# Post-norm decoder trunk, two layers: front transfers, token-major units, router order and the last block of each expert rearranged

## The chip, the cores and the metric

The kernel runs on one core of one Trainium2 chip. The metric is the time of one execution on the device in microseconds (us), the median of three. TensorE multiplies matrices and writes PSUM, VectorE and ScalarE do elementwise work, GpSimd issues indirect transfers, and SyncE's queue issues nearly all loads.

## What is computed

A hybrid trunk of D_MODEL 1024 runs over 256 tokens and two layers. x is float32, and every large product must be of about float32 accuracy.

```python
x <- LayerNorm(ALPHA * x + TokenMixer(x))
x <- LayerNorm(ALPHA * x + ChannelMixer(x))   # layer 0: dense SwiGLU; layer 1: top-2-of-8 SwiGLU experts
hcat = x @ w_in      # q, kv, gates | conv | retention q, k, v, g | merge gates
y = native sparse attention, short gated convolution, multi-scale retention, each projected, gated, summed, projected
```

D_FF is 3584 for the dense layer and for each of the eight experts. The router's logits are x @ moe_router (1024 x 8); each token goes to its two largest, with the softmax of the two as weights. The sparse attention has compressed keys and values: blocks of 32 tokens at stride 16, with a position encoding added, go through a small MLP.

## The kernel before

**Weights.** The weights are one stream of tiles ("subs") of 128 x 2048 float32, 1 MB each, in the order of use. SyncE loads them into six raw slots and waits, for each, until the tile six before has been split. ScalarE rounds a tile to w_hi (two instructions of 1024 columns, L892 and L893) and VectorE subtracts to get w_lo (L1205, L1208), into three ring slots. Activations are split in the same way (xT_hi and xT_lo, act_hi and act_lo), and every product is three matmuls: high x high, high x low, low x high. A split waits until TensorE has used the tile three before. Every engine works in the order in which its program is written.

**Layers.** norm(n) normalises the tokens, in two tiles of 128 (t = 0, 1). to_features(n) transposes them on TensorE (L419) into feature-major xT. stay_busy(k) issues k dummy matmuls (L407) where TensorE would wait. A mixer is 46 steps s, one per sub: projection units (fm_unit: weights 128x128 stationary, xT moving, 256 token columns, lines 361 to 363), four compression steps (L462, L463) that read the z pieces of key and value, branch projections and the output projection. Attention and retention work stands between the two halves of the units. Values must be token-major for attention and retention; they are computed feature-major and transposed: values_to_tokens (L471, four transposes a layer), ret_values (L579, eight a layer), each followed by a ScalarE copy.

**Front.** SyncE issues x, the identity, subs 0 and 1, three transfers of constants, then subs 2 to 5. Sub 0 is split in quarters (L899, L1218), after x is transposed.

**Router.** After norm(3), router_logits takes the product with wr2 (the router's high and low columns, 16 in all) as stationary, adds the two parts with a second small product (log2_ps), and counts with products against a lower triangle and ones (L752 to L756). VectorE's routing() finds the maxima, the masks, the weights (after ScalarE's exponential), the positions, the picks of item 0 (L1662), and the extra items for experts with more than 128 tokens; n_items = 8 plus these. gather_first (L764) then gathers item 0's rows by matmul.

**Experts.** Each item is seven blocks of 512 hidden columns. A block has four gate and up subs (up_half, L375 to L377: 128 tokens stationary, 512 weight columns moving), four transposes of the hidden block (L805), a split of it into hT_hi (ScalarE, L1116) and hT_lo (VectorE, L1691), and a down product over two subs. In blocks 0 to 5 the transposes stand behind the next block's gate; the last block is:

```python
n = i * NB + (NB - 1)
hidden_transposes(n)
gathered(i + 1)
down(n, s0 + (FFN - 2), MOE0 + 4, False, True)
```

gathered transposes the next item's rows (L779), which GpSimd has gathered by an indirect transfer (L1191) during the item. The result y is split (L1152, L1720) and scattered by matmul (L846, L847) in the next item, and VectorE adds it to acc (L1713).

## Time and profile before

| | |
|---|---|
| Median of three runs | 1862.42 us (1861.42 to 1862.79) |
| Profiled execution | 1861.52 us, its span 1859.7 us |
| Granted TensorE clock, mean | 0.996 |
| Busy: TensorE, VectorE, ScalarE, GpSimd | 1825.2, 1464.5, 1177.4, 45.2 us |
| Moved by DMA | 511 MB, 275 GB/s |

Times are microseconds from the start of the span. A matmul's row shows the time from its start to the end of its results; matmuls overlap, so the step from one start to the next is what one costs. The stages: front to 30, layer 0's mixer to 302, its dense part to 547, layer 1's mixer to 848, router to 863, eight items to 1839, scatter, norm and output to the end.

### The profile page before, as it was taken

Reading aid. Unit: us, or ns where it says so; the run is one execution under the profiler, and the core shown is the slowest. Engines: PE = TensorE matmul, PEld = TensorE weight load, DVE = VectorE, ACT = ScalarE, POOL = GpSimd, SP = SyncE. Lnnn points to the kernel's source line nnn. Section 1 sums busy time; section 2 is a strip of 40 time slices with the busy share of each in tenths; the row PEclk is TensorE's granted clock in tenths of the full one; section 3 lists DMA queues with packets and bytes.
Section 4 is the critical chain, followed back from the end, with each engine's and each line's share of the span. In section 5 each row is a group of like instructions: output and inputs, shape, how many; then the busy total and the mean of one; then the engine's idle time right before and its main releaser. Section 6 shows DMA issues by size and latency. Waiting matters only on the chain.

```text
span 1859.7 us, 29640 instructions
## 1 busy us (share of the span) xinstructions
PE 1825.2 (98%) x10921; PEld 1588.7 (85%) x10925; DVE 1464.5 (79%) x1697; ACT 1177.4 (63%) x1448; POOL 45.2 (2%) x15
## 2 busy tenths in 40 slices
PE   8999999999999999999999999999999999999995
PEld 7999998999989999996888888888888888888884
DVE  5685577544567665768999989999999999999998
ACT  6554444444447444445777787787787877777874
POOL 0000000000000000000101001000010010100100
PEclk9999999999999999999999999999999999999998
DMA  9444445555537333455999999999999999999994
GB/s 384 182 159 137 163 178 182 183 192 190 180 136 269 140 139 137 160 201 192 370 375 350 380 350 375 371 342 385 372 352 379 346 377 375 335 387 368 361 368 172
DMA packets 71870, 511.07 MB, mean 275 GB/s; under 512 B 8064, under 2 KB 8192, under 8 KB 10880
## 3 DMA queue, kind: packets, MB, share of 16 engines
q1 hardware_dynamic: 68944, 498.10, 70.9%
q10 hardware_dynamic: 1280, 6.32, 0.9%
q0 software_dynamic: 1584, 5.77, 0.9%
q8 instruction: 46, 0.75, 0.2%
q14 instruction: 16, 0.13, 0.0%
HBM read 508.06 MB, written 2.10 MB: 274 GB/s over the span
## 4 chain that ended last, share of the span: by engine, by line
PE 95%; DVE 3%; DMA 1%; ACT 1%; issue 0%; SPq 0%; DVEq 0%
PE PS L375 19%; PE PS L377 18%; PE PS L376 18%; PE PS L361 11%; PE PS L362 10%; PE PS L363 10%; PE PS L805 1%; DMA raw<-wstream 1%; PE PS L531 1%; PE PS L563 1%; PE PS L546 1%; DVE X L1260 0%; PE PS L846 0%; PE PS L847 0%; PE PS L541 0%; DVE bst L1230 0%
## 5 line engine op out<-in xcount | busy, mean ns | idle before, releaser
L1205 DVE TENSOR_TENSOR w_lo<-raw,w_hi 128x1024 fp32r<-128x1024 f32 x471 | 575.7, 1222 | 229.9 <-ACT w_hi L892 229.0
L892 ACT ACTIVATE w_hi<-raw 128x1024 fp32r<-128x1024 f32 x471 | 499.1, 1060 | 282.2 <-PE PS L377 210.1
L1208 DVE TENSOR_TENSOR w_lo<-raw,w_hi 128x1024 fp32r<-128x1024 f32 x471 | 574.0, 1219 | 0.0
L893 ACT ACTIVATE w_hi<-raw 128x1024 fp32r<-128x1024 f32 x471 | 493.1, 1047 | 0.0
L361 PE MATMUL PS<-xT_hi,w_hi 128*128 128x256 f32 x1408 | 404.2, 287 | 0.2 <-DVE w_lo L1208 0.2
L362 PE MATMUL PS<-xT_lo,w_hi 128*128 128x256 f32 x1408 | 398.2, 283 | 0.0
L363 PE MATMUL PS<-xT_hi,w_lo 128*128 128x256 f32 x1408 | 398.2, 283 | 0.0
L375 PE MATMUL PS<-w_hi,xT_hi 128*128 128x512 f32 x896 | 355.0, 396 | 1.5 <-DVE xT_lo L1677 1.5
L377 PE MATMUL PS<-w_hi,xT_lo 128*128 128x512 f32 x896 | 349.5, 390 | 0.0
L376 PE MATMUL PS<-w_lo,xT_hi 128*128 128x512 f32 x896 | 348.9, 389 | 0.0
L361 PEld LDWEIGHTS PS<-xT_hi,w_hi 128*128 128x128 f32 x1408 | 269.6, 192 | 10.3 <-issue 8.2
L362 PEld LDWEIGHTS PS<-xT_lo,w_hi 128*128 128x128 f32 x1408 | 269.8, 192 | 0.2
L363 PEld LDWEIGHTS PS<-xT_hi,w_lo 128*128 128x128 f32 x1408 | 269.8, 192 | 0.0
L375 PE MATMUL PS<-w_hi,act_hi 128*128 128x512 f32 x624 | 244.6, 392 | 5.0 <-DVE act_lo L1691 5.0
L376 PE MATMUL PS<-w_lo,act_hi 128*128 128x512 f32 x624 | 243.0, 389 | 0.0
L377 PE MATMUL PS<-w_hi,act_lo 128*128 128x512 f32 x624 | 242.9, 389 | 0.0
L375 PEld LDWEIGHTS PS<-w_hi,xT_hi 128*128 128x128 f32 x896 | 168.2, 188 | 38.9 <-DVE w_lo L1208 4.2
L377 PEld LDWEIGHTS PS<-w_hi,xT_lo 128*128 128x128 f32 x896 | 168.1, 188 | 35.9
L376 PEld LDWEIGHTS PS<-w_lo,xT_hi 128*128 128x128 f32 x896 | 168.5, 188 | 33.2
L375 PEld LDWEIGHTS PS<-w_hi,act_hi 128*128 128x128 f32 x624 | 117.1, 188 | 32.8 <-issue 6.8
L377 PEld LDWEIGHTS PS<-w_hi,act_lo 128*128 128x128 f32 x624 | 117.2, 188 | 24.6
L376 PEld LDWEIGHTS PS<-w_lo,act_hi 128*128 128x128 f32 x624 | 117.1, 188 | 23.5
(266 smaller groups left out, 1429.8 us busy)
## 6 DMA issues: line engine op xcount, KB each, us to landing
raw<-wstream SPq DMA_DIRECT2D x472, 1024.0 KB, 6.7
soft<-ln ACTq DMA_DIRECT2D x4, 1024.0 KB, 5.6
X<-x SPq DMA_DIRECT2D x1, 1024.0 KB, 4.9
x_rows<-X ACTq DMA_DIRECT2D x1, 1024.0 KB, 5.0
out<-X ACTq DMA_DIRECT2D x2, 512.0 KB, 3.7
cst<-consts SPq DMA_DIRECT2D x1, 910.0 KB, 10.5
sm<-small SPq DMA_DIRECT2D x1, 729.0 KB, 12.3
rg<-constb SPq DMA_DIRECT2D x1, 337.0 KB, 10.9
```

The costliest lines, as they stand in the source:

```text
L361: mm(o, wh, rhs_hi[:, k, :], start=(k == 0), stop=False)
L362: mm(o, wh, rhs_lo[:, k, :], start=False, stop=False)
L363: last = mm(o, wl, rhs_hi[:, k, :], start=False, stop=(k == nk - 1))
L375: mm(o, lh, wh, start=(first and n == 0), stop=False)
L376: mm(o, lh, wl, start=False, stop=False)
L377: last = mm(o, ll, wh, start=False, stop=(final and n == len(ks) - 1))
L531: last = mm(o[par][:, i, 0:w], query(NR * g + 2 * i + par, qt), kT[par * DH:(par + 1) * DH, a, g, 0:w], start=False, stop=(i == 1), skip_g ...
L546: last = nc.tensor.transpose(PS[:, TB + kb, r * P:(r + 1) * P], prob[:, r, kb * P:(kb + 1) * P], ident)
L892: activate(w_hi[:, at % RING, 0:SUB // 2], src[:, 0:SUB // 2], ACT.Copy).then_inc(half_done, 1)
L893: activate(w_hi[:, at % RING, SUB // 2:SUB], src[:, SUB // 2:SUB], ACT.Copy).then_inc(hi_done, 1)
L1205: v.tensor_tensor(w_lo[:, at % RING, 0:SUB // 2], src[:, 0:SUB // 2], w_hi[:, at % RING, 0:SUB // 2], ALU.subtract)
L1208: v.tensor_tensor(w_lo[:, at % RING, SUB // 2:SUB], src[:, SUB // 2:SUB], w_hi[:, at % RING, SUB // 2:SUB], ALU.subtract).then_inc(lo_done, 1)
```

## The change

1. SyncE issues the identity first, x in two transfers, sub 0 in four, and the constants behind sub 3 in four transfers, with the position encoding (pos_in) behind sub 2. Sub 0's quarters are split as they land; VectorE does the first two between its xT_lo pieces.
2. Units 4, 16 and 17 (attention values, retention values) are computed token-major by tm_unit: xT stationary, 256 weight columns moving. The transposes of values and the ScalarE copies behind them go. The columns of w_in are reordered, so that unit 3 holds both keys and unit 4 both values.
3. The logits are computed by token: xT stationary, wr2 moving, with the high part of the first tokens before the second tokens' transposes. The dummies are recounted (12 to 9 before x, 2 and 8 new in the front, 16 to 9 in norm(3), 2, 9 and 8 to 7 and 4 in the router).
4. In routing, counts and picks come before the weights; one weight split is moved from norm(3) to behind the picks; the extras go to GpSimd; acc and the zero y go to ScalarE; gather_first is in two halves around the load of n_items; the first expert's first tile waits for the first half of the rows alone.
5. In each item's block 5 the down product issues the transposes of block 6 between its two subs; their split goes to hL_hi and hL_lo, ahead of the last weight split of that block on ScalarE and VectorE. One weight split stands ahead of two additions at the item's start.

```diff
+TOKEN_UNITS = (4, 16, 17)
...
-            sp.dma_start(X[:, :, :], x.rearrange("(t p) d -> p t d", p=P)).then_inc(x_in, 16)
-            sp.dma_start(ident, consts[:, C_ID:C_ID + P]).then_inc(x_in, 16)
-            for t in range(RAW):
+            sp.dma_start(ident, consts[:, C_ID:C_ID + P]).then_inc(id_in, 16)
+            for t in range(TT):
+                sp.dma_start(X[:, t, :], x[t * P:(t + 1) * P, :]).then_inc(x_in[t], 16)
+            for c in range(4):
+                at = slice(c * SUB // 4, (c + 1) * SUB // 4)
+                sp.dma_start(raw[:, 0, at], wstream[0][:, at]).then_inc(landed[0] if c == 3 else part_in[c], 16)
+            for t in range(1, RAW):
                 sp.dma_start(raw[:, t], wstream[t]).then_inc(landed[t], 16)
-                if t == 1:
+                if t == 2:
+                    sp.dma_start(sm[:, 0, 0:S_B1], small[0][:, 0:S_B1]).then_inc(pos_in, 16)
+                if t == 3:
                     sp.dma_start(cst[:, P:C_W], consts[:, P:C_W]).then_inc(const_in, 16)
                     sp.dma_start(cstf, constb).then_inc(const_in, 16)
-                    sp.dma_start(sm[:, :, :], small.rearrange("l p c -> p l c")).then_inc(const_in, 16)
+                    sp.dma_start(sm[:, 0, S_B1:S_W], small[0][:, S_B1:S_W]).then_inc(const_in, 16)
+                    sp.dma_start(sm[:, 1, :], small[1]).then_inc(const_in, 16)
...
+            def tm_unit(bank, slot, middle=None):
+
+                for t in range(TT):
+                    if t and middle:
+                        middle()
+                    o, tok = PS[:, bank, t * T:(t + 1) * T], slice(t * P, (t + 1) * P)
+                    for k in range(DK):
+                        at = slice(k * 2 * P, (k + 1) * 2 * P)
+                        mm(o, xT_hi[:, k, tok], w_hi[:, slot, at], start=(k == 0), stop=False)
+                        mm(o, xT_hi[:, k, tok], w_lo[:, slot, at], start=False, stop=False)
+                        last = mm(o, xT_lo[:, k, tok], w_hi[:, slot, at], start=False, stop=(k == DK - 1))
...
                     if n == 0:
-                        pe.wait_ge(x_in, 32)
+                        if t == 0:
+                            pe.wait_ge(id_in, 16)
+                        else:
+                            stay_busy(2)
+                        pe.wait_ge(x_in[t], 16)
                     elif t == 1:
-                        stay_busy(16)
+                        if n == 3:
+                            router_high(0)
+                        stay_busy(9 if n == 3 else 16)
                     for k in range(DK):
                         if n and k % 4 == 0:
                             pe.wait_ge(norm_rdy, 2 * TT * (n - 1) + 2 * t + k // 4 + 1)
...
                                                    X[:, t, k * P:(k + 1) * P], ident)
                         if k % 4 == 3:
                             last.then_inc(norm_ps, 1)
-                if n:
-                    stay_busy(3)
+                stay_busy(3 if n else 8)
...
+                    if u in TOKEN_UNITS:
+                        tm_unit(PA[u % 2], (base + s) % RING, lambda: attention_between(s)).then_inc(sub_used, 1)
+                        return
...
-                    for a in range(2):
-                        for t in range(TT):
-                            nc.tensor.transpose(PS[:, TB + 1, (2 * a + t) * P:(2 * a + t + 1) * P],
-                                                vT[:, a, t * P:(t + 1) * P], ident)
...
-                    for h in range(RH):
-                        last = nc.tensor.transpose(PS[:, MB, h * P:(h + 1) * P], rvT[:, h, t * P:(t + 1) * P], ident)
-                    last.then_inc(rvt_ps, 1)
...
+            def router_high(t):
+                if t == 0:
+                    pe.wait_ge(wr_rdy, 1)
+                pe.wait_ge(xT_hi_rdy, TT * 2 * 3 + 2 * t + 2)
+                for k in range(DK):
+                    mm(logits[:, t, :], xT_hi[:, k, t * P:(t + 1) * P], wr2[:, k, :], start=(k == 0), stop=False)
+
             def router_logits():
-                pe.wait_ge(wr_rdy, 1)
-                pe.wait_ge(xT_hi_rdy, TT * 2 * 4)
-                pe.wait_ge(xT_rdy, TT * 2 * 3 + 1)
-                for k in range(DK):
-                    mm(PS[0:2 * NE, 0, 0:T], wr2[:, k, :], xT_hi[:, k, :], start=(k == 0), stop=False)
-                pe.wait_ge(xT_rdy, TT * 2 * 4)
-                for k in range(DK):
-                    last = mm(PS[0:2 * NE, 0, 0:T], wr2[:, k, :], xT_lo[:, k, :], start=False, stop=(k == DK - 1))
+                router_high(1)
+                for t in range(TT):
+                    for k in range(DK):
+                        if k % 4 == 0:
+                            pe.wait_ge(xT_rdy, TT * 2 * 3 + 2 * t + k // 4 + 1)
+                        last = mm(logits[:, t, :], xT_lo[:, k, t * P:(t + 1) * P], wr2[:, k, :], start=False,
+                                  stop=(k == DK - 1))
                 last.then_inc(log_ps, 1)
-                stay_busy(2)
-                pe.wait_ge(logT_rdy, 1)
-                for t in range(TT):
-                    last = mm(PS[:, 1, t * NE:(t + 1) * NE], logT[:, t * P:(t + 1) * P], fold8, start=True, stop=True)
-                last.then_inc(log2_ps, 1)
-
-                stay_busy(9)
+                stay_busy(7)
                 pe.wait_ge(cnt_in, 1)
                 m = [chosen_b[:, t, :] for t in range(TT)]
                 mm(PS[:, 0, 0:NE], before, m[0], start=True, stop=True)
...
                 mm(PS[:, 0, NE:2 * NE], ones, m[0], start=False, stop=True)
                 mm(PS[:, 0, 2 * NE:3 * NE], ones, m[0], start=True, stop=False)
                 mm(PS[:, 0, 2 * NE:3 * NE], ones, m[1], start=False, stop=True).then_inc(cnt_ps, 1)
-                stay_busy(8)
-
-            def gather_first():
-
-                pe.wait_ge(pick_rdy, 1)
-                for k in range(DK):
+                stay_busy(4)
...
+                gather_first(0)
                 pe.wait_ge(table_rdy, 1)
                 n_items = pe.value_load(table[0:1, NX + 1:NX + 2], min_val=NE, max_val=NI)
+                gather_first(1)
...
+                        if h and ahead:
+                            hidden_transposes(n + 1)
...
+                    pe.wait_ge(xe_rdy, i * 2 + 1)
+                    up_half(s0, MOE0, 0, 0)
                     pe.wait_ge(xe_rdy, i * 2 + 2)
-
-                    up_half(s0, MOE0, 0, 0)
                     up_half(s0 + 1, MOE0 + 1, 0, 1)
                     scatter(i)
                     up_half(s0 + 2, MOE0 + 2, 1, 0)
                     up_half(s0 + 3, MOE0 + 3, 1, 1)
                     body(i * NB, s0 + 4, MOE0 + 4, i)
-                    with pe.Fori(1, NB - 1) as b:
+                    with pe.Fori(1, NB - 2) as b:
                         body(i * NB + b, s0 + b * 6 + 4, MOE0 + 4)
-                    n = i * NB + (NB - 1)
-                    hidden_transposes(n)
+                    body(i * NB + (NB - 2), s0 + (FFN - 8), MOE0 + 4, last=True)
                     gathered(i + 1)
-                    down(n, s0 + (FFN - 2), MOE0 + 4, False, True)
+                    down(i * NB + (NB - 1), s0 + (FFN - 2), MOE0 + 4, False, True, lhs_last)
...
+            stay_busy(9)
...
+                    if n == 3:
+                        high(n, 2 * t)
+                        high(n, 2 * t + 1)
...
+            def high(n, b):
+                act.wait_ge(norm_ps, 4 * n + b + 1)
+                t, c = divmod(b, 2)
+                activate(xT_hi[:, 4 * c:4 * c + 4, t * P:(t + 1) * P],
+                         PS[:, NORM_BANKS[b], :].rearrange("p (k t) -> p k t", k=4), ACT.Copy).then_inc(xT_hi_rdy, 1)
 
...
-                        activate(V[:, :, :, :].rearrange("p a t c -> p (a t c)"), PS[:, TB + 1, :],
-                                 ACT.Copy).then_inc(v_rdy, 1)
-                    if s in (22, 24):
-                        t = (s - 22) // 2
-                        act.wait_ge(rvt_ps, TT * l + t + 1)
-                        activate(rv[:, t, :], PS[:, MB, :], ACT.Copy).then_inc(rv_rdy, 1)
...
+                def hidden_last(n):
+                    act.wait_ge(et_ps, n + 1)
+                    activate(hL_hi, PS[:, YB, :].rearrange("p (k t) -> p k t", k=4), ACT.Copy).then_inc(ehT_hi, 1)
+
+                def body(n, k, s, item=None, last=False):
                     for c in range(6):
+                        if c == 5 and last:
+                            hidden_last(n + 1)
...
+            activate(acc, X[:, :, :], ACT.Copy, scale=ALPHA).then_inc(acc_rdy, 1)
+            activate(y_hi, cst[:, 0:D], ACT.Copy, scale=0.0).then_inc(y_hi_rdy, 2)
+            activate(y_lo, cst[:, 0:D], ACT.Copy, scale=0.0).then_inc(y_rdy, 2)
...
+            pool.wait_ge(table_rdy, 1)
+            link(g.tensor_tensor(pr, tri8, over.unsqueeze(1).broadcast_to([P, NE, NE]), ALU.mult))
+            rank = sums(pr)
+            g.tensor_scalar(past, pos, float(1 - P), None, ALU.add)
+            for j in range(NX):
+                last = g.tensor_scalar(sel[:, j, :], rank, float(j), None, ALU.is_equal)
+            link(last)
+            link(g.tensor_tensor(sel, sel, wide, ALU.mult))
+            g.tensor_tensor(named, sel, iota8.unsqueeze(1).broadcast_to([P, NX, NE]), ALU.mult)
+            pool.wait_ge(wts_rdy, 1)
+            for t in range(TT):
+                for n, of in enumerate((past, wgt)):
+                    last = g.tensor_tensor(chosen[n][t], sel, of[:, t, :].unsqueeze(1).broadcast_to([P, NX, NE]),
+                                           ALU.mult)
+            link(last)
+            total = sums(every)
+            for t in range(TT):
+                g.tensor_scalar(slots[:, t, NE:NI], total[:, (1 + 2 * t) * NX:(2 + 2 * t) * NX], -1.0, None, ALU.add)
+                g.tensor_copy(wts[:, t, NE + 1:NI + 1], total[:, (2 + 2 * t) * NX:(3 + 2 * t) * NX])
+            g.tensor_copy(table[0:1, 0:NX], total[0:1, 0:NX]).then_inc(table_rdy, 1)
...
+                        if n == 0 and b >= 2:
+                            first_part(b - 2)
                     if n:
-                        for t in range(2 if n < 3 else 1):
+                        for t in range(2 if n < 3 else 0):
...
+                        v.tensor_copy(V[:, :, :, :].rearrange("p a t c -> p t a c"),
+                                      pa(4).rearrange("p t (a c) -> p t a c", a=2)).then_inc(dve_free, 1)
...
+                    if l == 0 and s == 4:
+                        dve.wait_ge(const_in, 16 * 4)
+                        v.tensor_copy(cb[:, :], cstf).then_inc(const_rdy, 1)
...
-                v.tensor_scalar(acc, X[:, :, :], ALPHA, None, ALU.mult).then_inc(acc_rdy, 1)
                 v.memset(wts[:, :, 0], 0.0)
                 link(v.memset(slots[:, :, NI], -1.0))
-                dve.wait_ge(log2_ps, 1)
-                link(v.tensor_copy(lg, PS[:, 1, 0:TT * NE].rearrange("p (n k) -> p n k", n=TT)))
+                dve.wait_ge(log_ps, 1)
+                link(v.reduce_sum(lg, logits.rearrange("p t (h e) -> p t e h", h=2), AX_X))
...
+                link(v.tensor_tensor(ch, m1, m2, ALU.add))
+
+                pos, wgt = slots[:, :, 0:NE], wts[:, :, 1:NE + 1]
+                over, count, po = route[:, 160:168], route[:, 184:185], at(144, TT, NE)
+                dve.wait_ge(cnt_ps, 1)
+                link(v.scalar_tensor_tensor(po, PS[:, 0, 0:TT * NE].rearrange("p (n k) -> p n k", n=TT), 1.0, ch,
+                                            ALU.add, ALU.mult))
+                link(v.tensor_scalar(pos, po, -1.0, None, ALU.add))
+                picks_first()
                 v.tensor_tensor(route[:, 98:100], mx[:, :, 1], mx[:, :, 0], ALU.subtract).then_inc(router_exp, 1)
+                link(v.tensor_scalar(over, PS[:, 0, 2 * NE:3 * NE], float(P), None, ALU.is_gt))
+                link(v.reduce_sum(count, over, AX_X))
+                v.tensor_copy(table[0:1, NX:NX + 1], count[0:1, :])
+                v.tensor_scalar(table[0:1, NX + 1:NX + 2], count[0:1, :], float(NE), None,
+                                ALU.add).then_inc(table_rdy, 1)
+                split(MOE0 + 1)
+                gather(0)
...
+                v.tensor_tensor(wgt, w1, w2, ALU.add).then_inc(wts_rdy, 1)
...
+                        if c == 5 and last:
+                            lower_last(n + 1)
...
+                    split(MOE0 + 5, i * NB)
                     add_scattered(i, (0, 1))
-                    split(MOE0 + 5, i * NB)
```

## Rows read from the trace of the kernel before

**Rows 1.** The page, busy us of TensorE and VectorE (share of the span).

```profile
PE 1825.2 (98%) x10921; PEld 1588.7 (85%) x10925; DVE 1464.5 (79%) x1697; ACT 1177.4 (63%) x1448; POOL 45.2 (2%) x15
```

**Rows 2.** Waits of TensorE (whole), ScalarE (experts): us in total, times, longest.

```profile
PE PS L375 <- DVE act_lo L1691: 5.0, 8, 0.6
PE PS L332 <- DVE w_lo L1218: 2.6, 1, 2.6
...
PEld PS L361 <- issue: 9.7, 28, 0.4
...
PEld PS L375 <- DVE w_lo L1208: 6.6, 21, 0.4
...
ACT w_hi L892 <- PE PS L377: 159.2, 249, 1.4
```

**Rows 3.** Busy us by window, clock, DMA share, GB/s: front and experts.

```profile
10.00:30.00 20.00, 16.70 (x133) 16.17 (x134) 15.67 (x22) 14.35 (x20) 0.00 (x0) 1.00 1.02 417
863.50:1840.00 976.50, 971.11 (x4416) 798.51 (x4416) 897.30 (x887) 766.77 (x839) 41.85 (x8) 1.00 0.94 359
```

**Rows 4.** Timeline of the front: start, us, what, [idle before, releaser].

```profile
1.18 5.30 PE L407 MATMUL PS<-cb 128*128 128x512 bf16 x12 [1.18 <-DVE cb L1751]
...
7.65 2.48 DVE L1279 TENSOR_TENSOR xT_lo<-PS,xT_hi 128x512 fp32r<-128x512 f32 x4 [6.50 <-ACT xT_hi L916]
...
18.48 1.06 ACT L892 ACTIVATE w_hi<-raw 128x1024 fp32r<-128x1024 f32 x1 [5.43 <-DMA raw<-wstream]
...
21.07 2.64 ACT L948 ACTIVATE act_hi<-PS 64x256 fp32r<-64x256 f32 x4
...
22.58 2.41 DVE L1355 TENSOR_TENSOR act_hi<-PS,act_hi 64x256 fp32r<-64x256 f32 x4
...
25.14 0.32 PE L462 MATMUL PS<-w_hi,act_hi 128*82 128x256 f32 x1 [2.21 <-DVE act_hi L1355]
...
27.44 0.38 PE L361 MATMUL PS<-xT_hi,w_hi 128*128 128x256 f32 x1 [0.22 <-DVE w_lo L1208]
```

**Rows 5.** Timeline of TensorE around the first tokens' retention transposes, layer 0.

```profile
165.10 0.28 PE L362 MATMUL PS<-xT_lo,w_hi 128*128 128x256 f32 x1
165.22 0.29 PE L363 MATMUL PS<-xT_hi,w_lo 128*128 128x256 f32 x1
165.34 0.60 PE L579 MATMUL PS<-cst,bufC 128*128 128x128 f32 x4
...
165.90 0.28 PE L362 MATMUL PS<-xT_lo,w_hi 128*128 128x256 f32 x1
```

**Rows 6.** Timeline of the router.

```profile
843.80 3.23 PEld L407 LDWEIGHTS PS<-cb 128*128 128x128 bf16 x16
...
849.77 1.07 PE L738 MATMUL PS<-xT_hi,wr 128*16 128x256 f32 x8
...
852.90 1.22 DVE L1586 TENSOR_SCALAR merged<-X 128x2048 f32<-128x2048 f32 x1
...
854.19 0.17 DVE L1590 COPY route<-PS 128x16 f32<-128x16 f32 x1
...
858.12 3.84 PE L764 MATMUL PS<-rv,X 128*128 128x128 f32 x32 [0.28 <-DVE rv L1662]
...
863.46 0.49 PE L375 MATMUL PS<-w_hi,xT_hi 128*128 128x512 f32 x1 [1.50 <-DVE xT_lo L1677]
```

**Rows 7.** Timeline of TensorE at the end of item 1.

```profile
977.40 0.60 PE L805 MATMUL PS<-cst,tmp 128*128 128x128 f32 x4
977.84 1.04 PE L779 MATMUL PS<-cst,G 128*128 128x128 f32 x8
979.49 0.49 PE L375 MATMUL PS<-w_hi,act_hi 128*128 128x512 f32 x1 [0.62 <-DVE act_lo L1691]
979.82 0.40 PE L376 MATMUL PS<-w_lo,act_hi 128*128 128x512 f32 x1
```

**Rows 8.** VectorE's weight splits while GpSimd works, 1129 to 1137: min/median/max ns.

```profile
L1205 DVE TENSOR_TENSOR w_lo<-raw,w_hi x4: 1216/1218/1220, 1129.5 to 1136.9; 128x1024 fp32r<-128x1024 f32 x4
```

199 lines of the change are left out of this document (83 added, 116 removed).

## Prediction, made before the result was known

> **What bounds the kernel now.** I read the page first. TensorE is busy 98% of the span, VectorE 79% [rows 1], so time is to be had in two ways only: fewer matmul instructions, or fewer moments in which TensorE waits. The list of TensorE's waits names the moments [rows 2]: 2.6 us before the first matmul of layer 0 (L332), 2.2 us before the first compression matmul (L462, in [rows 4]), and eight waits of 0.6 us for act_lo (L1691), one in each of the eight items that this input has. Around the router TensorE also runs dummy matmuls (L407) that stand for waiting. DMA moves 417 GB/s in the front and is at its limit there, 359 GB/s in the experts [rows 3]. ScalarE's waits before a split in the experts (159 us) are all for TensorE, none for a transfer [rows 2], so DMA sets nothing there. The profiled execution took 1861.52 us, of which the span is 1859.7; the median of three runs is 1862.42, 0.9 above it.
>
> **Front.** The third weight tile (sub 2) is queued behind the constants and reaches ScalarE at 18.48, after 5.43 us of waiting [rows 4]. ScalarE and VectorE work in program order, so the z pieces that compression reads queue behind this tile's split and end at 25.0; TensorE, done with sub 1 at 22.8, waits for them. The change puts the constants (0.93 + 0.35 + 0.75 MB) behind sub 3. At 0.417 MB per us sub 2 lands 4.8 us earlier, near 13.6, and its split is over by 17. First I follow sub 0. VectorE does four xT_lo and four w_lo quarters at 0.6 us each, from 7.65 to 12.5. x in halves and nine dummies for twelve (they take 5.3 us from 1.18) let the first transposes start near 5.1, 1.2 earlier, but the second half of x lands about where x landed, and the new order (xT_lo, quarter, xT_lo, quarter) has VectorE wait for ScalarE's first quarter: I get 9.3 for the start of the first quarter and 12.2 for the end of the last. That is 0.3 us gained. Unit 0 then ends at 16.6, sub 1 takes 48 matmuls at 0.12 = 5.8 us and ends at 22.4, the z pieces need 3.9 us from the end of unit 0 (21.07 to 25.0 before) and are there at 20.8, compression takes 1.9 us, and sub 3 starts at 24.35 (its split ends near 23.2) where it started at 27.44. Gain 3.1 us. The bounds: 4.0 if 1.2 us of the earlier start come through, 1.5 if the smaller transfers make sub 0 late by as much. The eight dummies after the transposes fill a wait (1.6 us at 0.20 each, of the 2.6). The change issues 17 transfers on SP's queue ahead of sub 6 where there were 11; that queue runs ahead of the data, whose bytes are the limit there [rows 3]. The constants land near 20.4 and are first wanted by VectorE after sub 4, near 35, and by ScalarE not before the gelu; behind VectorE's wait stand its splits, but it has been met by then. A matmul stream after 2.6 us of idling still runs at 0.12 per 256 columns, while the twelve first dummies take 0.43 per 512, twice the 0.20 that they take at 844 [rows 4, 6]: the 1.2 GHz level is left before 6.3 and did not come back over a longer idle stretch than the changed kernel has (the clock column shows 1.00 in both stretches of [rows 3]).
>
> The Trainium skill (DMA: Bandwidth & Descriptors, Bandwidth) says to batch transfers to 1 MiB and speaks against cutting x and sub 0 up. In the rows the queue holds several transfers at once and moves 417 GB/s, so I do not follow it here; by its table's 138 GB/s for 64 KB pieces, an estimate, sub 0 would land about 5 us later and the front's gain would be near 1.
>
> **Mixers.** Four transposes for V and eight for the retention values go in each layer, with one ScalarE copy each behind them. Four transposes shift the matmul stream by 0.44 us (second matmul behind them at 165.90, where 165.46 was due) [rows 5]; V's take 0.5. Per layer 0.5 + 2 x 0.44 = 1.4, for two layers 2.8 us; with the issue gaps that stand at some of these places 3.3, without V's share of the switch 2.4. The three token-major units (4, 16, 17) issue the same 48 matmuls with 128 stationary and 256 moving columns; the trace has 256 moving columns at 0.12 and 512 at 0.226 whichever operand is the weight, so I cost them at nothing. ScalarE's k copies grow by 0.4 us behind unit 3, VectorE's work behind unit 4 shrinks by 1.5 us; both lie beside a unit's 5.8 us of matmuls, and if ScalarE had no room the cost would be that 0.4 once per layer.
>
> **Router.** Before [rows 6], the logits are there at 851.9, but VectorE first does a weight split (850.63 to 853.0) and acc (to 854.1), and reads them at 854.19. Now acc is ScalarE's, the split comes later, and the logits come in one step: eight high products for the first tokens are hidden before the second tokens' transposes (with nine dummies in place of sixteen: 0.9 + 1.8 us from 844.7, in time for the 847.6 at which the tokens are ready). Then 24 products of 128 stationary columns at 0.114 (the step of the 32 gather matmuls) from 849.75 end at 852.5, and VectorE starts at 852.65 (1.5 earlier). Moving counts and picks ahead of the weights' chain takes 1.0 more from VectorE's path: counts wanted at +1.6, back at +1.9, two links and the picks to +2.9. The gather starts at 855.55, not 858.12: 2.57 gained. It took 3.84 us, and TensorE waited 1.5 more for the two evictions. In two halves, the first half is evicted while the second runs; the first expert's first tile wants only it. TensorE's end of gather is 855.55 + 3.84 + 0.3 for the register load in between (the gap that VectorE shows after its own) = 859.7, against 863.46: 3.75 gained. VectorE's moved split (2.3 us, 856.3 to 858.5) ends just before it is wanted. Part is given back. In items 2 to 8 VectorE runs without a pause from 9.4 us into the item and makes TensorE wait three times, 21 waits and 6.6 us in the seven items, 0.94 each, less some 0.08 that each restart shows anyway: 0.7 [rows 2]. Item 1 had more head start and no such wait; with ScalarE's table loads and VectorE's weights chain now behind the gather (splits from 863.3, 3.6 us after TensorE; 3.7 in item 2) it joins them. Net gain 3.05. Bounds: 3.8 if it doesn't join, 1.65 if the register load costs TensorE 1.7 us, the idle that its weight loads show there. The split of tile 5 ahead of two additions only moves the wait: VectorE's queue is as long. ScalarE's acc, y_hi and y_lo (2.0 + 1.0 + 1.0 us from 850) end before its exponential is wanted.
>
> **Experts.** At each item's end four transposes of the hidden block and eight of the next rows cost 1.36 us at 0.1135, and then TensorE stands still until ScalarE and VectorE have split the block: the second matmul of the last down is at 979.82, where 977.40 + 1.36 + 0.23 = 978.99 was due [rows 7]. The wait is 0.83 us. The change puts the four transposes between the halves of the down before; the halves last 2.7 us, and the hidden block is ready at 973.5, 0.9 before it is wanted. ScalarE now waits for them at 975.3 with one weight split queued behind (0.9 later), VectorE ends that split at 979.3, and TensorE wants it at 981.4. The slack is 2 us. At the item's end both engines stand relative to TensorE as before. Gain 8 x 0.83 = 6.6; at least 3.9 if the extra switch costs what switches with an issue gap show, 9.7 us over 28 = 0.35 each [rows 2]; at most 6.8.
>
> **Sum.** 3.1 + 2.8 + 3.05 + 6.6 = 15.55 us. 1861.52 - 15.55 = 1846.0, and with the 0.9 of the median 1847 us. The low ends (1.5, 2.4, 1.65, 3.9) give 1853, the high ends (4.0, 3.3, 3.8, 6.8) 1844.5.
>
> **Rivals.**
> - *GpSimd slows VectorE.* 22 small instructions move to GpSimd and run beside VectorE's weight splits, which gate TensorE there. If each holds VectorE for what a like one takes on VectorE (0.18 us), the 12 after the weights cost 2.2 us: 1849. Against it: VectorE's splits at 1129.5 to 1136.9 run beside a 5.2 us GpSimd instruction at 1.22 us each, as everywhere [rows 8]; but that one makes descriptors. 0.10.
>  The Trainium skill (GPSIMD Engine Reference, Specifications) says that the two share SBUF interfaces, with contention where VectorE has two SBUF inputs, as the splits have. By that rule this rival would come true; no row here shows it.
> - *Front gains little.* The cut transfers or the order of quarters cost what the constants give: 1849.5. 0.12.
> - *The item's wait comes back.* ScalarE's new wait holds its splits by more than the 2 us of slack, and the tile ring makes TensorE wait as long elsewhere: 1853.6. Against it: the timing above; for it: VectorE is busy 92% of an item. 0.09.
> - *Token-major matmuls are slower.* Six units x 48 = 288 matmuls. If they took the 0.226 of the 512-column ones, the kernel would be 31 us slower than forecast, 1878; it turns slower than before from 0.054 us extra each. Nothing in the rows has this shape, though both its sides are there. 0.04.
>
> **How the numbers follow.** My forecast has 0.65 (1844.5 to 1849). The range 1843.5 to 1854 takes in the first three rivals and the bounds, and leaves out the last rival and unknown mishaps. A change below 0.2% (3.7 us) can't be told from none. Faster: all but the last rival and something unseen, 0.91; same 0.04; slower 0.05.
>
> **What would show it.** TensorE's first sub 3 matmul near 24.4 and no wait above 0.3 us between 12 and it; no L471 and L579 transposes; the first gather matmul about 7.9 us after the second tokens' first transpose of norm 3 (10.4 before); item period 121.2 instead of 122.05; no wait for act_lo at the item's end. I am wrong if VectorE's splits in the first item grow beyond 1.23 us, if the item's period stays, or if a token-major matmul steps by more than 0.12.

## The result, and the profile after

The changed kernel takes 1847.3 us (median of four executions, 1845.76 to 1848.3), the one before 1862.61 beside it on the same chip: ratio 0.9919, 95% interval 0.9904 to 0.9934. The forecast was 1847. The profiled execution took 1848.0 us with a span of 1846.1, so between the two profiles lie 13.5 us where the medians lie 15.3 apart; why is told below. One execution of the run f1_no_empty_alone below (2366.4 us, mean clock 0.71) and one of the kernel before beside it (2253.37 us, 0.75) were slow executions and are in no other number. The marks of TensorE and GpSimd in the two timelines divide the 13.6 us of span:

| mark | before | after | ahead by |
|---|---|---|---|
| TensorE's first sub 3 matmul | 27.44 | 25.18 | 2.26 |
| norm 1, first tokens' transposes | 301.97 | 298.41 | 3.56 |
| norm 2, second tokens' transposes | 553.08 | 549.53 | 3.55 |
| norm 3, second tokens' transposes | 847.72 | 842.90 | 4.82 |
| first expert matmul | 863.46 | 855.69 | 7.77 |
| GpSimd's row gather in item 2 | 1007.69 | 999.76 | 7.93 |
| the same in item 8 | 1739.98 | 1726.93 | 13.05 |
| end of VectorE's last instruction | 1854.44 | 1840.57 | 13.87 |
| end of the span | 1859.7 | 1846.1 | 13.6 |

The page's busy line, beside [rows 1]: TensorE lost 4.3 us of work, dummies included, and the rest of the span's 13.6 us, 9.3, is waiting.

```profile
PE 1820.9 (99%) x10905; PEld 1587.3 (86%) x10905; DVE 1457.5 (79%) x1670; ACT 1179.3 (64%) x1441; POOL 56.1 (3%) x37
```

The list of waits, beside [rows 2]. The eight waits for the hidden block's split are gone; of the first matmul's 2.6 us, 1.3 are left; 16 waits for w_lo take the same 6.6 us as 21 did: two in each of eight items now, three in each of seven before, when item 1 had none. L371 to L373 are the feature-major matmuls now, L384 to L386 the token-major ones, L398 to L400 the 512-column ones, L448 the transposes.

```profile
PEld PS L371 <- issue: 8.2, 24, 0.4
PEld PS L398 <- DVE w_lo L1273: 6.6, 16, 0.6
...
PE PS L342 <- DVE w_lo L1282: 1.3, 2, 0.9
```

Windows of the front and the router (columns as in [rows 3]; the two numbers before the last are the granted clock and DMA's busy share). In the front DMA is busy but moves only 161 GB/s for two us; in the router the granted clock falls to 0.50, TensorE's 1.2 GHz level, while TensorE is busy all the time; it stays there for 3.4 us, from 847.2 to 850.6.

```profile
4.00:6.00 2.00, 1.71 (x12) 1.11 (x11) 0.00 (x0) 0.32 (x1) 0.00 (x0) 1.00 0.99 371
6.00:8.00 2.00, 2.00 (x15) 1.41 (x14) 1.67 (x3) 1.78 (x5) 0.00 (x0) 1.00 0.93 161
8.00:10.00 2.00, 1.65 (x10) 0.83 (x7) 1.60 (x3) 0.90 (x3) 0.00 (x0) 1.00 1.06 397
10.00:30.00 20.00, 18.82 (x150) 17.92 (x149) 14.71 (x19) 14.47 (x20) 0.00 (x0) 1.00 1.02 416
...
846.00:848.00 2.00, 2.00 (x17) 2.00 (x17) 0.00 (x0) 2.00 (x3) 0.00 (x0) 0.80 1.04 315
848.00:850.00 2.00, 2.00 (x6) 0.65 (x6) 1.50 (x12) 1.98 (x3) 0.00 (x0) 0.50 1.02 354
850.00:852.00 2.00, 1.91 (x12) 0.72 (x10) 0.79 (x5) 0.30 (x1) 0.00 (x0) 0.84 0.48 201
```

The timeline, by stretches: the front beside [rows 4], a token-major unit, the router beside [rows 6], the switch inside the down product of item 1's block 5 beside [rows 7].

```profile
9.69 1.97 ACT L920 ACTIVATE w_hi<-raw 128x512 fp32r<-128x512 f32 x3 [1.10 <-DMA raw<-wstream]
...
11.10 0.39 PE L342 MATMUL PS<-xT_hi,w_hi 128*128 128x256 f32 x1 [0.93 <-DVE w_lo L1282]
...
13.52 1.06 ACT L913 ACTIVATE w_hi<-raw 128x1024 fp32r<-128x1024 f32 x1 [1.86 <-DMA raw<-wstream]
...
14.61 1.22 DVE L1270 TENSOR_TENSOR w_lo<-raw,w_hi 128x1024 fp32r<-128x1024 f32 x1 [2.10 <-ACT w_hi L913]
...
20.14 2.59 DVE L1422 TENSOR_TENSOR act_hi<-PS,act_hi 64x256 fp32r<-64x256 f32 x4
...
23.90 1.22 DVE L1273 TENSOR_TENSOR w_lo<-raw,w_hi 128x1024 fp32r<-128x1024 f32 x1
...
25.18 0.39 PE L371 MATMUL PS<-xT_hi,w_hi 128*128 128x256 f32 x1 [0.23 <-DVE w_lo L1273]
...
40.54 0.28 PE L384 MATMUL PS<-w_hi,xT_hi 128*128 128x256 f32 x1
40.66 0.28 PE L385 MATMUL PS<-w_lo,xT_hi 128*128 128x256 f32 x1
40.78 0.28 PE L386 MATMUL PS<-w_hi,xT_lo 128*128 128x256 f32 x1
...
844.88 1.06 PE L753 MATMUL PS<-wr,xT_hi 128*128 128x16 f32 x8
845.79 2.27 PE L761 MATMUL PS<-wr,xT_lo 128*128 128x16 f32 x16
847.91 3.01 PE L430 MATMUL PS<-cb 128*128 128x512 bf16 x7
850.76 0.17 PE L767 MATMUL PS<-chosen_b,cb 128*128 128x8 bf16 x1
...
852.10 3.84 PE L780 MATMUL PS<-rv,X 128*128 128x128 f32 x32 [0.19 <-DVE rv L1704]
855.69 0.48 PE L398 MATMUL PS<-w_hi,xT_hi 128*128 128x512 f32 x1
...
967.57 0.60 PE L825 MATMUL PS<-cst,tmp 128*128 128x128 f32 x4
967.92 0.47 PE L398 MATMUL PS<-w_hi,act_hi 128*128 128x512 f32 x1
...
970.76 1.03 PE L795 MATMUL PS<-cst,G 128*128 128x128 f32 x8
971.55 0.48 PE L398 MATMUL PS<-w_hi,xT_hi 128*128 128x512 f32 x1
```

What the reader is to see: ScalarE waits 1.10 us for sub 0's second quarter and 1.86 for sub 1; VectorE waits 2.10 behind it, and from there its splits and the z pieces follow one another until sub 3's split ends at 25.12, which releases sub 3's first matmul; token-major matmuls step by 0.12; seven dummies take 3.01 us, 0.43 each, and the counts behind them, ready to start at 849.74 (VectorE's chosen_b ends), start at 850.76; the first expert matmul follows the gather without a gap; TensorE doesn't wait at either switch at the end of the item.

### The profile page after: what moved, and what is told of

Read it like the earlier page. It is cut to its first block, busy times and chain, and to the rows that moved or that the text cites. A ratio compares the mean times of both kernels' runs of the same rounds, so it can differ in the third digit from the quotient of the medians.

```text
span 1846.1 us, 29565 instructions
## 1 busy us (share of the span) xinstructions
PE 1820.9 (99%) x10905; PEld 1587.3 (86%) x10905; DVE 1457.5 (79%) x1670; ACT 1179.3 (64%) x1441; POOL 56.1 (3%) x37
## 4 chain that ended last, share of the span: by engine, by line
PE 87%; DVE 6%; ACT 3%; issue 2%; DMA 1%; SPq 0%; DVEq 0%; ACTq 0%
PE PS L398 16%; PE PS L400 16%; PE PS L399 16%; PE PS L371 10%; PE PS L372 10%; PE PS L373 10%; DVE w_lo L1273 2%; DVE w_lo L1270 1%; PE PS L825 1%; DVE merged L1762 1%; ACT w_hi L913 1%; PE PS L557 1%; PE PS L589 1%; PE PS L384 1%; DMA raw<-wstream 1%
## 5 line engine op out<-in xcount | busy, mean ns | idle before, releaser
L398 PE MATMUL PS<-w_hi,xT_hi 128*128 128x512 f32 x960 | 380.0, 396 | 0.6 <-DVE w_lo L1273 0.2
L371 PE MATMUL PS<-xT_hi,w_hi 128*128 128x256 f32 x1312 | 376.3, 287 | 0.2 <-DVE w_lo L1273 0.2
L400 PE MATMUL PS<-w_hi,xT_lo 128*128 128x512 f32 x960 | 374.5, 390 | 0.0
L399 PE MATMUL PS<-w_lo,xT_hi 128*128 128x512 f32 x960 | 373.8, 389 | 0.0
L372 PE MATMUL PS<-xT_lo,w_hi 128*128 128x256 f32 x1312 | 371.1, 283 | 0.0
L373 PE MATMUL PS<-xT_hi,w_lo 128*128 128x256 f32 x1312 | 371.0, 283 | 0.0
L371 PEld LDWEIGHTS PS<-xT_hi,w_hi 128*128 128x128 f32 x1312 | 251.3, 192 | 9.1 <-issue 6.8
L373 PEld LDWEIGHTS PS<-xT_hi,w_lo 128*128 128x128 f32 x1312 | 251.4, 192 | 0.0
L398 PE MATMUL PS<-w_hi,act_hi 128*128 128x512 f32 x560 | 219.7, 392 | 0.0
L400 PE MATMUL PS<-w_hi,act_lo 128*128 128x512 f32 x560 | 218.1, 389 | 0.0
L399 PE MATMUL PS<-w_lo,act_hi 128*128 128x512 f32 x560 | 218.0, 389 | 0.0
L398 PEld LDWEIGHTS PS<-w_hi,xT_hi 128*128 128x128 f32 x960 | 180.3, 188 | 39.3 <-DVE w_lo L1273 4.0
L400 PEld LDWEIGHTS PS<-w_hi,xT_lo 128*128 128x128 f32 x960 | 180.2, 188 | 38.4
L398 PEld LDWEIGHTS PS<-w_hi,act_hi 128*128 128x128 f32 x560 | 105.2, 188 | 23.7 <-DVE w_lo L1273 2.6
L400 PEld LDWEIGHTS PS<-w_hi,act_lo 128*128 128x128 f32 x560 | 105.1, 188 | 22.1
```

The source lines that it names most:

```text
L371: mm(o, wh, rhs_hi[:, k, :], start=(k == 0), stop=False)
L372: mm(o, wh, rhs_lo[:, k, :], start=False, stop=False)
L373: last = mm(o, wl, rhs_hi[:, k, :], start=False, stop=(k == nk - 1))
L398: mm(o, lh, wh, start=(first and n == 0), stop=False)
L399: mm(o, lh, wl, start=False, stop=False)
L400: last = mm(o, ll, wh, start=False, stop=(final and n == len(ks) - 1))
```

## The experiments

Twelve kernels ran; e5_halves, e8_pool_load and e9_no_empty also carry the two dummies of e7_between. Their times stand beside runs of the kernel before on the same chip (medians 1861.3 to 1861.7). Since executions of one kernel differ by 0.6 to 4.3 us, I read each stage between marks, which repeat from profile to profile where nothing was changed (from norm 2's transposes of the second tokens to norm 3's of the first 288.66 or 288.67 in all; from the first expert matmul to VectorE's end 984.80 to 984.95; from the front's end to norm 1 273.1 to 273.4), and the whole only as a second witness.

**1. The last block as it was** (e1_last_block).

```diff
-                    with pe.Fori(1, NB - 2) as b:
+                    with pe.Fori(1, NB - 1) as b:
                         body(i * NB + b, s0 + b * 6 + 4, MOE0 + 4)
-                    body(i * NB + (NB - 2), s0 + (FFN - 8), MOE0 + 4, last=True)
+                    n = i * NB + (NB - 1)
+                    hidden_transposes(n)
                     gathered(i + 1)
-                    down(i * NB + (NB - 1), s0 + (FFN - 2), MOE0 + 4, False, True, lhs_last)
+                    down(n, s0 + (FFN - 2), MOE0 + 4, False, True)
```

(ScalarE and VectorE likewise.)

> The changed kernel with the last block as it was: its four transposes stand ahead of the last down product again, everything else as changed. Theory (the wait for the split of the hidden block was worth 0.83 us per item): the item's period goes from 121.19 back to 122.05 us, TensorE's eight waits of about 0.6 us for act_lo return, and the profiled execution takes 6.8 us more, 1854.8. Rival (the items became shorter by something else in the change, such as the weight split that now stands ahead of two additions): the period stays near 121.2 and the time within 1 us of 1848.0.

1854.62 us (ratio 0.9963, 0.9949 to 0.9977). The wait is back (list of waits), and GpSimd's gathers of items 2 and 3 start 122.05 us apart, where the changed kernel has 121.16 (its timeline follows):

```profile
PE PS L398 <- DVE act_lo L1733: 4.9, 8, 0.6
```

```profile
998.97 5.20 POOL L1256 DMA_INDIRECT G<-x_rows,rows  x1 [116.61 <-DVE rows L1714]
1121.02 5.23 POOL L1256 DMA_INDIRECT G<-x_rows,rows  x1 [116.85 <-DVE rows L1714]
```

```profile
999.76 5.20 POOL L1256 DMA_INDIRECT G<-x_rows,rows  x1 [115.73 <-DVE rows L1714]
1120.92 5.24 POOL L1256 DMA_INDIRECT G<-x_rows,rows  x1 [115.96 <-DVE rows L1714]
```

From the first expert matmul to VectorE's end it takes 991.69 us, with the last block changed 984.88: 6.8 us, 0.85 per item. The rival falls. The run gives one number more. From the first expert matmul to the gather in item 2 it takes 144.93 us, in the kernel before 144.23: with the item itself as before, item 1 is 0.70 slower. That is the 0.7 us which the forecast charged for item 1 joining the others' waits, and the waits are there: 1.1 us for w_lo in item 1 of this run and of the changed kernel, none in item 1 of the kernel before.

**2. Values by transposes again** (e2_values). TOKEN_UNITS is empty, and the twelve transposes per layer, their copies and the old order of columns are back.

```diff
-TOKEN_UNITS = (4, 16, 17)
+TOKEN_UNITS = ()
...
+                    if s in (23, 25):
+                        ret_values((s - 23) // 2)
```

> The changed kernel with units 4, 16 and 17 feature-major again and the twelve transposes per layer back. Theory (the transposes' own TensorE time, 1.3 to 1.4 us per layer, token-major matmuls free): from TensorE's first sub 3 matmul to the first transposes of norm 1 it takes 274.5 us where the changed kernel takes 273.2, and the whole 2.6 to 2.8 us more, 1850.7. Rival (half of what layer 0 gained came from the constants' later arrival or the other moved work in it, not from the transposes): the stretch is 273.8 at most and the whole takes 1.3 us more.

1851.49 us (0.9944, 0.9927 to 0.9961). From the first sub 3 matmul (25.46) to norm 1's transposes (299.98) it takes 274.52 us, the kernel before 274.53, the changed one 273.23; over layer 1 289.96, 289.96 and 288.66. The transposes cost 1.30 us per layer, and nothing else in the mixers gained or lost. The whole is 4.2 us over the changed kernel's median, where 2.6 to 2.8 was expected; VectorE's end lies 3.03 later, of which 2.6 are the transposes and 0.3 the front, and the intervals of the two ratios overlap.

**3. The front: what the cuts do** (e3_sub0_whole, e5_halves, f4_constants_only).

```diff
-            for c in range(4):
-                at = slice(c * SUB // 4, (c + 1) * SUB // 4)
-                sp.dma_start(raw[:, 0, at], wstream[0][:, at]).then_inc(landed[0] if c == 3 else part_in[c], 16)
+            sp.dma_start(raw[:, 0], wstream[0]).then_inc(landed[0], 16)
```

(All four quarters of ScalarE then wait for landed[0]. The diff is that of e3; e5 has two transfers, f4 also x in one.)

> The changed kernel with sub 0 in one transfer, ScalarE's first quarter waiting for all of it. Theory (the 256 KB quarters are slow: 161 GB/s from 6 to 8 us where the kernel before moved 426, so every later tile landed about 2 us later than forecast): the rate between 6 and 8 us is near 400, sub 1 is at ScalarE by 12.5 instead of 13.52, TensorE's 0.93 us wait inside unit 0 is gone, and its first sub 3 matmul comes 0.4 to 0.8 us before 25.18. Rival (the dip belongs to the start of the weight stream or to x, not to the cut): the rate dips as much, sub 1 comes at 13.5, TensorE's first matmul at 10 instead of 9.46, and sub 3's is at 25.2 to 25.7.

> As the kernel with dummies between the low products, and sub 0 in two transfers of 512 KB (rows of 4 KB, as each half of x) instead of four of 256 KB. Theory (what slows the queue is the 2 KB row of a quarter): between 6 and 8 us the rate is near 400 GB/s, as with sub 0 whole; ScalarE has its first quarter by 8.3, TensorE starts unit 0 near 9.9, sub 1 is at ScalarE by 12, and the first sub 3 matmul comes at 24.3 to 24.6, where the changed kernel had 24.5 to 25.5 in four profiles and sub 0 whole 25.0. Rival (any cut of sub 0 costs the queue as much as it brings): the rate dips below 250 again and sub 3 starts at 25.0 or later.

> The changed kernel with x in one transfer and sub 0 in one transfer: of the front's edits only the later constants, the quarters' order on VectorE and the dummies are left. Theory (nearly all of the front's gain is the constants' move; the cuts give and take about the same): TensorE's first sub 3 matmul comes at 25.1 to 25.6, 1.8 to 2.3 us before the 27.44 of the kernel before. Rival (x in two halves carries much of it, as its transposes start 1.2 us earlier): sub 3 starts at 26.0 or later.

| | GB/s, 6 to 8 us | sub 1 at ScalarE | first matmul | first sub 3 matmul |
|---|---|---|---|---|
| quarters (changed kernel) | 161 | 13.52 | 9.46 | 25.18 |
| sub 0 whole | 432 | 11.63 | 10.65 | 25.03 |
| sub 0 in halves | 252 | 13.29 | 11.03 | 25.40 |
| x and sub 0 whole | 408 | 11.61 | 11.03 | 25.40 |

Windows of e3_sub0_whole, then of e5_halves:

```profile
6.00:8.00 2.00, 2.00 (x18) 1.78 (x17) 1.02 (x2) 1.43 (x3) 0.00 (x0) 1.00 1.03 432
```

```profile
6.00:8.00 2.00, 2.00 (x15) 1.79 (x15) 0.92 (x2) 1.23 (x3) 0.00 (x0) 1.00 1.00 252
```

The theory is right about the queue: with sub 0 whole the dip is gone and sub 1 is there 1.9 us sooner. Its consequence for the end was wrong: unit 0 starts 1.2 us later, so the earlier sub 1 finds TensorE behind. The halves miss what was expected of them and do what the rival said: they dip too, and sub 3 starts no earlier. So the 2 KB row isn't the whole cause: each half of x has the same 4 KB rows as the halves of sub 0, and between 4 and 6 us, when x is under way, e3 moved 414 GB/s and e5 356. Why a cut sub 0 moves slower stays open; in the ten profiles with quarters the rate between 6 and 8 us is 161 to 235 GB/s. f4 (one execution, 1847.47 us) came as expected (25.1 to 25.6).

Those ten profiles have sub 3's first matmul at 24.41 to 25.46, mean 24.83. The spread has one cause that every profile shows. In all ten, sub 3 starts 11.63 to 11.69 us after ScalarE gets sub 1 (12.73 to 13.82), whenever the first matmul was: VectorE's chain of the rows above. In e3, e5 and f4 it starts 14.37 us after TensorE's first matmul, whenever sub 1 came: TensorE's chain. The later of the two decides. The quarters let TensorE's chain begin early and VectorE's late; the whole tile does the reverse. With the first matmul at 9.46 and sub 1 at 11.6, sub 3 would start at 23.8, an estimate from these sums that no run tried. What stands: with both cuts undone 2.0 us of the gain are left (one profile); that is the constants' move with the new order behind it, and the cuts add 0.6 by the mean of ten. The times of e3 (1847.3, 0.9927) and e5 (1846.84, 0.9920) don't differ from the changed kernel's.

**4. Four dummies instead of seven** (e4_dummies4).

```diff
                 last.then_inc(log_ps, 1)
-                stay_busy(7)
+                stay_busy(4)
```

> The changed kernel with 4 dummies instead of 7 between the logits and the counts. Theory (the granted clock is 0.50 there after the products with 16 moving columns, a dummy takes 0.43 us, and seven of them hold the counts back from 849.75 to 850.76): the counts start at 849.75, the picks and the gather 1.0 us earlier (gather 851.1), and the whole takes 1.0 us less, 1847.0. Rival (the three dummies that go are what brings the clock back: counts come earlier but the granted clock is still 0.50 in the gather, whose 32 products then take up to twice their 0.114 us): TensorE's first expert matmul stays within 0.3 us of 855.69 or comes later.

The rival held. Counts no longer queue behind dummies, and the gather pays for it (timeline, then windows):

```profile
849.14 1.87 PE L430 MATMUL PS<-cb 128*128 128x512 bf16 x4
850.80 5.71 PE L780 MATMUL PS<-rv,X 128*128 128x128 f32 x32
856.26 0.48 PE L398 MATMUL PS<-w_hi,xT_hi 128*128 128x512 f32 x1
```

```profile
850.00:852.00 2.00, 2.00 (x9) 1.64 (x8) 1.93 (x9) 0.20 (x1) 1.04 (x1) 0.50 0.31 127
852.00:854.00 2.00, 2.00 (x12) 2.00 (x10) 1.14 (x2) 0.00 (x0) 1.78 (x3) 0.50 0.00 0
854.00:856.00 2.00, 2.00 (x15) 2.00 (x15) 0.69 (x1) 0.60 (x1) 1.59 (x7) 0.77 0.75 225
```

From the second tokens' transposes to the first expert matmul it takes 13.85 us, the changed kernel 12.79. The profiles of e1 and e3 show that it can be less with the changed kernel's instructions: 11.52 and 11.51, with the clock at 1.00 throughout. The clock falls in some executions and not in others. Here that costs 1.3 us with seven dummies behind, and 2.3 with four, where the clock is low for 6.8 us instead of 3.4; over the profiles with seven it costs 0.8 to 1.5. This is one profile with four dummies: by the medians (1847.08, 0.9920, 0.9904 to 0.9937) the kernel is as fast as the changed one, so the three dummies gain nothing and lose nothing that whole times show.

**5. What lets the clock fall?** (e7_between, f2_every_second, f3_dummies_first). One dummy ahead of each eight low products; one behind every second of the 24 products; and the norm's nine dummies moved:

```diff
                 for t in range(TT):
+                    stay_busy(1)
                     for k in range(DK):
```

```diff
                     elif t == 1:
+                        stay_busy(9 if n == 3 else 16)
                         if n == 3:
                             router_high(0)
-                        stay_busy(9 if n == 3 else 16)
```

> The changed kernel with one dummy matmul (512 moving columns) ahead of each token's eight low products, so that no run of products with 16 moving columns is longer than eight. In five profiles so far TensorE's granted clock fell to 0.50 during or right after the 24 products in three (changed kernel, values, dummies4) and stayed at 1.00 in two (last block, sub 0 whole), with the same instructions ahead of it. Theory (the long run of products with few columns lets the clock fall, in some executions): the clock stays at 1.00 here, from the second tokens' first transpose to the first expert matmul it takes 11.9 us (11.5 of the two undisturbed ones and 0.4 for the dummies) instead of 12.8, and the times of the executions spread less than the 2.5 us of the changed kernel. Rival (the fall has to do with what comes later or with chance, not with these products): it falls in this kernel or in the three others that carry the same two dummies as often, and the stretch takes 13.2.

> As the kernel with no empty gathers, and one dummy with 512 moving columns behind every second one of the router's 24 last products (12 dummies, 2.4 us at 0.20 each). In nine profiles of kernels with those products the clock fell in five, one dummy per eight products or none alike. Theory (the stream of 16-column products is what lets the clock fall, and one dummy per eight is too few): here no execution falls; all lie within 0.5 us of each other, near 1846.5, where the kernel without the dummies shows two groups 1.2 us apart, and the profile's clock is 1.00 throughout the router. Rival (the fall has another cause): some executions fall and cost 1.2 us more, as without.

> As the kernel with no empty gathers, and the nine dummies of norm 3 stand ahead of the first eight router products instead of behind them, so that TensorE doesn't stand idle for 0.83 us before these. Theory (the later 24 products alone let the clock fall): it falls as often as before, two groups of executions 1.2 us apart, and the rest of the router is as in the changed kernel. Rival (the idle and the eight products early in the norm are part of what the clock answers to): no execution falls, the clock is 1.00 throughout, and all executions lie within 0.5 us near 1843.9. Either way TensorE's transposes of the second tokens start when VectorE has their rows, within 0.1 us of now.

e7 took 1847.26 us (0.9924, 0.9910 to 0.9937), and its clock fell; it fell in one more (e9) of the four profiles that carry these two dummies, so the theory of e7 is refuted. Over all twelve profiles with at most one dummy per eight products the clock fell in six. f2: no fall in its profile, five executions within 0.6 us (1845.12 to 1845.7), median 1845.44 (0.9915, 0.9901 to 0.9929); twelve dummies cost 1.6 us, not 2.4, since they take the place of some of the waiting behind them. f3: no fall in the profile; four executions at 1843.50 to 1844.07 and one at 1846.41 with a lower mean clock (0.995 for 0.997); median 1843.8 (0.9909, 0.9895 to 0.9923). But the run below without any such edit also had no fall in its profile and no second group among its four executions, so five or four such executions prove little. Shown: in half of the profiles the clock falls during or right behind these products, while TensorE is busy; in the one profile of the kernel before, whose logits moved 256 columns (L738, [rows 6]), it stays at 1.00. Not shown: that the few columns are the cause; that stays open.

**6. GpSimd beside VectorE** (e8_pool_load).

```diff
+            link(g.memset(scratch[:, :], 0.0))
...
+            for _ in range(24):
+                link(g.tensor_tensor(scratch[:, 0:64], scratch[:, 0:64], scratch[:, 64:128], ALU.add))
             pool.wait_ge(rows_out, 16)
```

> As the kernel with dummies between the low products, and GpSimd adds 24 more dependent additions of 128x64 elements behind its part of the routing, beside VectorE's weight splits of the first item (their results are not used). Theory (GpSimd's work doesn't hold VectorE): the splits beside them take 1.20 to 1.24 us each, as all others, and the time is that of the kernel without the additions within 0.5 us. Rival (both share a port, and each GpSimd addition holds VectorE for its time): the splits beside them take 1.4 us or more, TensorE waits for w_lo in the first item, and the whole takes 2 us or more longer.

Between the two. In the changed kernel six half splits run beside the routing's instructions at 1.20 to 1.24 us, as in [rows 8]. In e8, 15 half splits run while the additions do: the ten that follow another split without a pause take 1.34, the five behind a pause 1.21 to 1.23 (one line of VectorE, 864.5 to 881, ns min/median/max; e8, then e7):

```profile
L1278 DVE TENSOR_TENSOR w_lo<-raw,w_hi x5: 1341/1343/1348, 865.1 to 878.7; 128x1024 fp32r<-128x1024 f32 x5
```

```profile
L1274 DVE TENSOR_TENSOR w_lo<-raw,w_hi x6: 1211/1224/1227, 863.5 to 879.4; 128x1024 fp32r<-128x1024 f32 x6
```

A split is held by 0.12 us, 10%, and not by the other's whole time. It is GpSimd that waits: an addition takes 0.32 us where VectorE has no split under way or starts one only at its end (10 of 24), and 1.18 to 1.37 beside a split (14 of 24), ending 0.18 after it. The routing's own instructions do the same in the changed kernel (timelines of GpSimd and VectorE):

```profile
857.13 0.23 POOL L1238 TENSOR_TENSOR route<-route 128x24 f32<-128x24 f32 x1
...
861.32 1.21 DVE L1273 TENSOR_TENSOR w_lo<-raw,w_hi 128x1024 fp32r<-128x1024 f32 x1
861.45 1.13 POOL L1249 COPY wts<-route 128x3 f32<-128x3 f32 x1
862.46 1.21 DVE L1270 TENSOR_TENSOR w_lo<-raw,w_hi 128x1024 fp32r<-128x1024 f32 x1
```

The copy of three columns ends at 862.58, 0.05 behind the split. The experts take 985.78 us to VectorE's end instead of 984.93; the ten held splits come to 1.2 us and can account for it, which isn't shown by itself. The whole takes 1847.8 us (0.9927, 0.9912 to 0.9942), 0.5 over e7's and within its interval. By the Trainium skill (GPSIMD Engine Reference, Specifications) the two contend where VectorE has two SBUF inputs; the trace agrees for a steady load, at that price, and for the change's 22 small instructions shows no cost to VectorE.

**7. The end of the kernel** (e9_no_empty, f1_no_empty_alone). GpSimd gathers rows for eleven items one after another; this input has eight. The last three gathers have nothing to fetch. The expectation of e9 calls their rows out of bounds, but by the code their row numbers are all 0 (no token is picked, and the number is a sum over picked tokens), and each moves 0.52 MB like the others.

```diff
-            for i in range(NI):
+            def fetch(i):
...
+            for i in range(NE):
+                fetch(i)
+            extra = pool.value_load(table[0:1, NX:NX + 1], min_val=0, max_val=NX)
+            with pool.If(extra > 0):
+                for i in range(NE, NI):
+                    fetch(i)
```

> As the kernel with dummies between the low products, and GpSimd issues the three row gathers of the extra items only when there are extra items (this input has none, and all their rows are out of bounds). In the profiles so far the span ends 5.7 to 6.6 us after GpSimd's last gather instruction and 4.4 to 6.8 us after VectorE's last one, and of the run with the last block undone the chain of waits ends in these gathers. Theory (the empty gathers, one after another, hold the end or hold back the last output transfer): the span ends 4.4 us or less after VectorE's last instruction, 1 us earlier than in the changed kernel on average (up to 2.4). Rival (the output transfer's own time sets the end): it ends 5.2 to 5.5 us after VectorE's last instruction and nothing is gained.

> The changed kernel, and GpSimd issues the three row gathers of the extra items only when there are extra items. With the dummies between the low products the same edit brought the span's end from 5.5 us (mean of nine profiles, 4.4 to 6.8) to 3.1 us after VectorE's last instruction. Theory: the two effects are separate, and without those two dummies (0.3 us) the executions fall in two groups, 1843.9 us where the clock stays and 1845.1 where it falls in the router, median 1844.5, 2.5 to 3 us under the changed kernel. Rival (the short end was chance): the span ends 5 us or more after VectorE's last instruction and the median is 1847.

From VectorE's last instruction to the end of the span it takes 3.05 to 3.10 us in all four kernels with this edit, where it took 4.4 to 6.8 in the ten others, the kernel before (5.3) included. What they hold back is the last output transfer, with which they share the DMA engines: its last byte moves 2.32 us after VectorE's end in the four, 3.35 to 5.34 in the ten, 4.43 in the changed kernel. Of e1 the chain of waits ends in the gathers themselves:

```profile
1833.62 4.48 DMA G<-x_rows,rows
1838.22 0.70 issue
1838.92 4.96 DMA G<-x_rows,rows
1843.99 0.70 issue
1844.69 1.23 POOL G L1256
```

e9: 1844.32 us (0.9907, 0.9892 to 0.9923); f1: 1844.31 (0.9908, 0.9892 to 0.9924). That is 2 us under the changed kernel by the ratios and 3 by the medians; the tail itself is 2.5 shorter on average (5.6 to 3.1). The tail is what shows the gain; the intervals of the ratios overlap with the changed kernel's (0.9904 to 0.9934). f3, the same with the dummies moved, has the lowest median, 1843.8; the intervals of the three don't tell them apart.

## Why the prediction was right

**Front**, forecast 3.1, measured 2.26 in the pair of profiles and 2.6 over ten. The mechanism is the forecast's (constants behind sub 3; compression no longer waits), the size was off by one sentence: "that queue runs ahead of the data, whose bytes are the limit there". Between 6 and 8 us DMA was busy and moved 161 GB/s; sub 0's second quarter came late (TensorE's second wait, 0.93), sub 1 at 13.5. The forecast had sub 3's split done near 23.2 and TensorE as the one that sets its start; the split was done at 25.12, because VectorE's chain begins with sub 1 (run 3). By the table of the Trainium skill (DMA: Bandwidth & Descriptors, Bandwidth) small transfers are slower, and the dip agrees with that. The forecast's estimate from it took the rate of 64 KB transfers for pieces of 256 KB and had sub 0 land 5 us later, with a front gain near 1; sub 1 came 1.9 us later than with sub 0 whole, and the front gained 2.26.

**Mixers**, forecast 2.8, measured 2.60: 1.30 per layer by run 2. The difference is small, and which of the twelve transposes was charged too much no run tells. Token-major matmuls step by 0.12, as costed.

**Router**, forecast 3.75, measured 2.95 in the profiled execution and 4.2 where the clock stays (from norm 3's second transposes to the first expert matmul 15.74 us before, 12.79 and 11.52 after). Two errors of opposite sign. The clock was taken as 1.00; it fell in half of the profiles (1.3 us in the profiled one). The end of the gather was put at its start plus 3.84 and 0.3 for the register load; the next matmul starts 3.59 behind the first product (3.84 is to the end of the last one's results), with no gap for the load, 0.55 better. With the clock at 1.00 the forecast's sign is met, the first gather matmul 7.9 us after the second tokens' first transpose (7.92 in e1 and e3); in the profiled execution it is 9.20. The giving back of 0.7 came as forecast (run 1).

**Experts**, forecast 6.6, measured 6.8 (run 1): 0.85 an item. Switching inside the down product costs no gap beyond the transposes' own time.

**Sum.** 2.26 + 2.60 + 2.95 + 6.8 - 0.7 = 13.9; VectorE's end moved by 13.87, and the span by 13.6, as the tail behind it is 0.3 longer in this pair. The profiled execution is one with the fall, and its front is 0.35 slower than the mean. With the front at 2.6 and the router at 2.95 to 4.2 the same sum gives 14.3 to 15.5, and the medians 15.3. The forecast's 15.55 lies at the upper end: its front was too high by 0.5, its mixers by 0.2, its experts too low by 0.2, and its router happened to lie between the two cases that it did not know of. The mechanisms held; that the total came within 0.3 us is luck in part.

**Rivals.** GpSimd's contention exists, but GpSimd bears nearly all of it: a split loses a tenth of its time under a steady load and nothing here. The front's small gain did not come. The item's wait did not return. Token-major matmuls are not slower.

## What to carry to other kernels

Divide a gain at marks that every profile has (a first matmul, a gather per item); that tells 0.3 us or less where whole times differ by 2. Where a mark itself wanders, as sub 3's first matmul did by 1 us, look for the event that it follows at a fixed distance. Dummy matmuls behind a stretch at risk are insurance: taking three away saved nothing, and in the one profile with four the stretch took 1.1 us more than in the one with seven, both with a fall. Before tuning the middle, look at what ends last: three gathers that did nothing cost more than the router's last microsecond.
